# Splitting one ScalarE copy in two and re-spacing the delta-rule levels of a two-block fp32 kernel

## The reference

```python
kk = jnp.einsum("bhncd,bhnjd->bhncj", k, k)
m = jnp.where(strict, beta[..., :, None] * kk * decay, 0.0) + jnp.eye(C, dtype=f32)
rhs = jnp.concatenate([v * beta[..., None], k * (beta * jnp.exp(gc))[..., None]], axis=-1)
sol = lax.linalg.triangular_solve(m, rhs, left_side=True, lower=True, unit_diagonal=True)
...
def step(state, inp):
    u = u0_c - jnp.einsum("bhcd,bhde->bhce", w_c, state)
    o = jnp.einsum("bhcd,bhde->bhce", qd_c, state) + jnp.einsum("bhcj,bhje->bhce", qk_c, u)
    state = cd_c[..., None, None] * state + jnp.einsum("bhcd,bhce->bhde", kd_c, u)
    return state, o
```

## Time and profile before

| | |
|---|---|
| median of 3 runs | 3284.47 us (3281.02 to 3286.4) |
| the profiled execution | 3288.24 us, its span 3286.4 us |
| TensorE matmuls busy | 3119.8 us (95% of the span) |
| VectorE, ScalarE, GpSimd busy | 48%, 26%, 51% |
| chain that ended last | PE 83%, DVE 12%, ACT 3% |
| trips 1 to 12 | about 430 to 1660 us of the span |
| mean DMA rate | 93 GB/s |

### The profile page before, as it was taken

One profiled execution on the slowest core, in us unless ns is written; L12 is line 12 of the kernel. 1 busy time (PEld: TensorE's weight loads), 2 busy tenths in 40 slices (PEclk: granted clock), 3 DMA queues, 4 the chain that ended last, 5 costly groups with the idle time before them and its releaser, 6 DMA issues.

```text
span 3286.4 us, 43215 instructions
## 1 busy us (share of the span) xinstructions
PE 3119.8 (95%) x15168; PEld 2545.6 (77%) x15168; DVE 1566.5 (48%) x2169; ACT 851.4 (26%) x1327; POOL 1684.4 (51%) x1748
## 2 busy tenths in 40 slices
PE   8999989999999999999799999999989999999996
PEld 7877778778778777787688887778768887778685
DVE  6721245555655556555622124344356666530723
ACT  5421133332333323333201011111123333310411
POOL 0255544444444344443357776566645555456774
PEclk9999999999999999999899999999999999999998
DMA  6322222212221221222242223222232212323221
GB/s 244 132 72 92 93 71 77 77 57 70 77 89 64 71 76 68 79 79 75 104 170 90 93 99 134 91 102 89 102 115 80 83 67 83 105 75 128 77 100 79
DMA packets 53527, 306.47 MB, mean 93 GB/s; under 512 B 5044, under 2 KB 7220, under 8 KB 21716
## 3 DMA queue, kind: packets, MB, share of 16 engines
q1 hardware_dynamic: 34528, 248.53, 21.6%
q10 hardware_dynamic: 18932, 57.00, 4.6%
HBM read 284.74 MB, written 20.77 MB: 93 GB/s over the span
## 4 chain that ended last, share of the span: by engine, by line
PE 83%; DVE 12%; ACT 3%; issue 1%; DMA 1%; ACTq 0%; DVEq 0%
PE gemm_ps L424 20%; PE gemm_ps L426 20%; PE gemm_ps L425 20%; DVE arena L859 7%; PE bankC L558 2%; DVE a_lo L859 2%; PE bankA L548 2%; PE gemm_ps L776 2%; PE gemm_ps L778 2%; PE gemm_ps L777 2%; PE bankA L732 2%; ACT arena L1590 2%; DVE arena L865 1%; PE bankB L579 1%; PE bankA L573 1%
## 5 line engine op out<-in xcount | busy, mean ns | idle before, releaser
L424 PE MATMUL gemm_ps<-a_hi,w_hi 128*128 128x512 f32 (+1 forms) x3472 | 1390.3, 400 | 24.1 <-DVE a_lo L859 14.4
L400 POOL CAST w_hi<-w_raw 128x512 fp32r<-128x512 f32 x872 | 538.8, 660 | 1555.1 <-issue 1393.6
L426 PE MATMUL gemm_ps<-a_hi,w_lo 128*128 128x512 f32 (+1 forms) x3472 | 1334.5, 384 | 0.0
L425 PE MATMUL gemm_ps<-a_lo,w_hi 128*128 128x512 f32 (+1 forms) x3472 | 1332.9, 384 | 0.0
L392 POOL TENSOR_TENSOR w_lo<-w_raw,w_hi 128x512 fp32r<-128x512 f32 x872 | 1149.5, 1349 | 4.3
L424 PEld LDWEIGHTS gemm_ps<-a_hi,w_hi 128*128 128x128 f32 x3472 | 659.6, 190 | 158.5 <-issue 24.0
L426 PEld LDWEIGHTS gemm_ps<-a_hi,w_lo 128*128 128x128 f32 x3472 | 656.7, 189 | 131.2
L425 PEld LDWEIGHTS gemm_ps<-a_lo,w_hi 128*128 128x128 f32 x3472 | 659.3, 190 | 121.8 <-issue 9.2
L859 DVE TENSOR_TENSOR arena<-gemm_ps,arena 128x512 f32<-128x512 f32 (+3 forms) x161 | 107.1, 665 | 606.1 <-PE gemm_ps L426 472.7
L1590 ACT ACTIVATE arena<-arena 128x512 f32<-128x512 f32 (+5 forms) x350 | 214.6, 613 | 410.7 <-DVE arena L859 396.0
L859 DVE RECIPROCAL arena<-arena 128x512 f32<-128x512 f32 (+2 forms) x70 | 172.7, 2468 | 249.9 <-ACT arena L1590 247.8
(11 more groups left out here) (168 smaller groups left out, 2571.3 us busy)
## 6 DMA issues: line engine op xcount, KB each, us to landing
w_raw<-w_stream SPq DMA_DIRECT2D x236, 1024.0 KB, 4.8
y_scratch<-arena ACTq DMA_DIRECT2D x20, 512.0 KB, 3.2
arena<-y_scratch ACTq DMA_DIRECT2D x13, 512.0 KB, 3.9
arena<-gc_scratch ACTq DMA_DIRECT2D x12, 512.0 KB, 5.8
arena<-x_t ACTq DMA_DIRECT2D x2, 2048.0 KB, 9.9
arena<-y_scratch ACTq DMA_DIRECT2D x1, 4096.0 KB, 24.5
x_scratch<-arena ACTq DMA_DIRECT2D x1, 4096.0 KB, 14.3
y_out<-arena ACTq DMA_DIRECT2D x4, 1024.0 KB, 3.9
```

Of the source, the lines that this page charges most:

```text
L400: pool.tensor_copy(part(w_hi, w, q), part(w_raw, w, q)).then_inc(pool_step, 1)
L424: pe.matmul(o, hi, a_hi[:, k, 0:width], start=(k == 0), stop=False)
L425: pe.matmul(o, hi, a_lo[:, k, 0:width], start=False, stop=False)
L426: last = pe.matmul(o, lo, a_hi[:, k, 0:width], start=False, stop=(k == KT - 1))
```

## The change

Four things.
1. The product T of a level is written to two PSUM banks, chunks 0 and 1 to bank A's first, 2 and 3 to its second (level 1 keeps both in the first, since the second is still being read). TensorE signals after each pair; ScalarE copies T in two 128x256 activations; `whole` waits for each half on its own.
2. The four column operations behind level 2 go from VectorE to ScalarE, at the head of `values`.
3. `DN_STEPS` gets other weights: `half` 0 in place of 1 everywhere, so that no dense block stands between `half` and `whole`; `values` 13 for 12; at level 5 `whole` 2 for 1 and `turn` 2 for 3; at level 6 `whole` 1 for 2; `head_out` 24 for 18.
4. The step counts per trip follow (57 for 61 and 24 for 20).

```diff
-DN_STEPS = ([("natural", 12), ("values", 12)]
-            + [(s, l, w) for l in range(1, LEVELS - 2) for s, w in (("half", 1), ("whole", 4))]
-            + [("half", LEVELS - 2, 1), ("whole", LEVELS - 2, 1), ("turn", 3)]
-            + [("half", LEVELS - 1, 1), ("whole", LEVELS - 1, 2), ("flip", 2), ("solved", 4)]
+DN_STEPS = ([("natural", 12), ("values", 13)]
+            + [(s, l, w) for l in range(1, LEVELS - 2) for s, w in (("half", 0), ("whole", 4))]
+            + [("half", LEVELS - 2, 0), ("whole", LEVELS - 2, 2), ("turn", 2)]
+            + [("half", LEVELS - 1, 0), ("whole", LEVELS - 1, 1), ("flip", 2), ("solved", 4)]
             + [(s, n, g) for n in range(NB) for s, g in (("rest", 2), ("output", 3))]
-            + [("head_out", 18)])
+            + [("head_out", 24)])
...
+        def half_bank(l, q):
+
+            return bankA[:, q if l > 1 else 0, :]
...
                     for n in range(NB):
-                        last = pe.matmul(quad(bankA)[:, 0, n, :], pair_n[:, n, :], inv_a[:, n, :],
+                        last = pe.matmul(half_bank(l, n // 2)[:, n * P:n * P + P], pair_n[:, n, :], inv_a[:, n, :],
                                          start=True, stop=True)
-                    last.then_inc(s["t1"], 1)
+                        if n % 2:
+                            last.then_inc(s["t1"], 1)
...
                     for n in range(NB):
+                        if n % 2 == 0:
+                            pe.wait_ge(s["t1_sbuf"], 2 * level_count(j, l) - 1 + n // 2)
...
-                    elif l == 2:
-                        op(v.tensor_copy, ke_scale[:, :, 0], cb[:, :, 3, 0])
-                        op(v.tensor_scalar, u_scale[:, :, 0], neg_br[:, :, 0], -1.0, None, ALU.mult)
-                        op(v.tensor_copy, u_scale[:, :, 1], kroot)
-                        op(v.tensor_scalar, neg_k, kroot, -1.0, None, ALU.mult)
...
+                    op(ke_scale[:, :, 0], cb[:, :, 3, 0], ACT.Copy)
+                    op(u_scale[:, :, 0], neg_br[:, :, 0], ACT.Copy, scale=-1.0)
+                    op(u_scale[:, :, 1], kroot, ACT.Copy)
+                    op(neg_k, kroot, ACT.Copy, scale=-1.0)
...
-                    op(chunks(T1, 0), bankA[:, 0, :], ACT.Copy, s["t1_sbuf"], level_count(j, step[1]))
+                    for q in range(2):
+                        done = 2 * level_count(j, step[1]) - 1 + q
+                        act.wait_ge(s["t1"], done if step[1] > 1 else 2 * level_count(j, 1))
+                        op(chunks(T1, 0)[:, q * 256:q * 256 + 256], half_bank(step[1], q)[:, q * 256:q * 256 + 256], ACT.Copy,
+                           s["t1_sbuf"], done)
```

More of the change, by code:

```diff
@@ L547, in dn_mix @@
                     for n in range(NB):
-                        last = pe.matmul(quad(bankA)[:, 0, n, :], pair_n[:, n, :], inv_a[:, n, :],
+                        last = pe.matmul(half_bank(l, n // 2)[:, n * P:n * P + P], pair_n[:, n, :], inv_a[:, n, :],
                                          start=True, stop=True)
-                    last.then_inc(s["t1"], 1)
+                        if n % 2:
+                            last.then_inc(s["t1"], 1)
                 elif step[0] == "whole":
                     l = step[1]
-                    pe.wait_ge(s["t1_sbuf"], level_count(j, l))
                     pe.wait_ge(s["inv_ready"], 2 * level_count(j, l))
@@ L1093, in dn_mix @@
                         op(v.tensor_tensor, dT[:, :, :, :], E[:, :, :, :], both(dTm), ALU.mult)
-                    elif l == 2:
-                        op(v.tensor_copy, ke_scale[:, :, 0], cb[:, :, 3, 0])
-                        op(v.tensor_scalar, u_scale[:, :, 0], neg_br[:, :, 0], -1.0, None, ALU.mult)
-                        op(v.tensor_copy, u_scale[:, :, 1], kroot)
-                        op(v.tensor_scalar, neg_k, kroot, -1.0, None, ALU.mult)
                     elif l == 3:
                         op(v.tensor_tensor, kd[:, :, :, :], both(by_chunk(bankB[:, 0, :])), by_row(kd_scale), ALU.mult)
-                    else:
+                    elif l == 4:
                         op(v.tensor_tensor, ke[:, :, :, :], both(by_chunk(bankB[:, 0, :])), by_row(ke_scale), ALU.mult,
@@ L1761, in dn_mix @@
                 elif step[0] == "half":
-                    act.wait_ge(s["t1"], level_count(j, step[1]))
                     if step[1] == 1:
                         act.wait_ge(s["dy_stored"], 16 * j + 16)
-                    op(chunks(T1, 0), bankA[:, 0, :], ACT.Copy, s["t1_sbuf"], level_count(j, step[1]))
+                    for q in range(2):
[3 more added lines that the diff above has]
+                           s["t1_sbuf"], done)
                 elif (step[0] == "whole" and step[1] < LEVELS - 2) or step[0] == "turn":
@@ L2158 @@
             + [("values", 0)])
-DN_VECTOR_STEPS = 61
-DN_SCALAR_STEPS = 20
+DN_VECTOR_STEPS = 57
+DN_SCALAR_STEPS = 24
 def kernel(**inputs):
```

## The result

| | before | after |
|---|---|---|
| median (4 runs each, side by side) | 3283.2 us | 3257.8 us (3255.16 to 3259.18) |
| ratio, 95% interval | | 0.9922 (0.991 to 0.9934) |
| the profiled execution, its span | 3288.24, 3286.4 us | 3257.62, 3255.8 us |
| start of trip 1, start of trip 12 | 429.74, 1557.21 us | 427.96, 1535.38 us |
| trip 1 | 111.8 us | 109.8 us |

The kernel became 25.4 us faster; 23 were forecast. The two profiled executions lie 30.6 us apart, and the place of each piece can be read: 1.8 us ahead of trip 1 (which the change doesn't touch), 2.0 in trip 1, 18.1 in trips 2 to 11, 8.8 from the start of trip 12 to the end. The distance of the medians, 25.4 us, is what the change is worth; the profiled execution of the kernel before is itself 5.0 us slower than its median here.

What follows compares the result with a forecast made beforehand. TensorE, busy 95% of the span, bounds the kernel; only its idle and half-clock time can be won. Trips -3, clock -14.6, first trip -2.5, last -2.5: about -23 us, from 3284.5 to 3261.5 us, range 3250 to 3277.

Steps and rivals of the forecast that it cites:

- level 1: Level 1, both copies behind all four products: 5.7 to 5.8 us against 5.98, one block less, +0.5 us a trip.
- level 2, level 4: Plain levels, `half` to next `half`: 0.62 us shorter, but one block of 0.675 must go elsewhere, +0.06 each.
- level 3: Level 3 without the column operations on VectorE: 2.12 us less, one block less, -1.45 us a trip.
- level 5: `half` to `turn` at level 5: 3.47 us against 4.03 with as many blocks, -0.55 us a trip.
- `turn` to `solved`: Stretch from `turn` to `solved`: 7.2 us against 8.81, three blocks (2.0) less, +0.4 us a trip.
- behind `solved` (`rest`): State update behind `solved`: no block ahead of `output` 2, so `rest` 3 waits a block more, +0.7 us a trip.
- trip 1: First trip: most of its 11.7 us excess comes ahead of level 1 and stays; -2.5 us for its level 3.
- trip 12: Last trip: the four column operations leave the stretch ahead of the wait for tile 0's bank, -2.5 us.
- The 14.6 us: Excess of ten trips, put down to the clock falling behind the gap ahead of level 4's `half`; all -14.6 us taken.
- Rival A: Levels 1 to 4: clock falls as often as before through several close gaps, the 14.6 us stay, 3276 us; chance 0.16.
- C: ScalarE becomes late, level 1 waits 1.6 us a trip, 19 us in all, 3281 us; chance 0.05.
- B: Levels 1 to 4 run at 1.2 GHz once every trip, 2.7 us each, 3294 us, 0.3% slower; chance 0.09.

Runs made afterwards that it cites:

- cols_split: Kernel after with the old `DN_STEPS` weights restored, split and moved column operations kept: 3222.33 us, ratio 0.9801 to the kernel before.
- undo_cols: Kernel after with the four column operations back on VectorE behind level 2: 3288.47 us, ratio 1.0007 to the kernel before.
- split_only: Kernel before with only T's split into two banks and two copies, old weights, columns on VectorE: 3286.23 us, ratio 0.9998.

## Why the prediction was right, and where it was off

Trip 3 by the prediction's steps; measured is the change of the stretch plus 0.675 us for each block taken out of it:

| step | predicted | measured |
|---|---|---|
| level 1 | +0.5 | 5.75 - 5.98 + 0.675 = +0.45 |
| level 2, level 4 | +0.06 each | 5.08 long: +0.08, +0.09 |
| level 3 | -1.45 | 6.18 - 8.20 + 0.675 = -1.35 |
| level 5 | -0.55 | 3.43 - 4.03 = -0.60 |
| `turn` to `solved` | +0.4 | 7.04 - 8.81 + 2.03 = +0.26 |
| behind `solved` (`rest`) | +0.7 | +0.73 |
| the trip | -0.3 | 100.11 to 99.76: -0.35 |
| trips 2 to 11 | -14.6 - 2.8 = -17.4 | -18.1 |
| trip 1 | -2.8 | -2.0 |
| trip 12 | -2.5 | -8.8 to the end |

**The steady trips** came out as worked out: the signs named (trips near 99.8 and alike, level 3 at 6.1, plain levels at 5.05, `rest` 3 waiting 1.4, clock at 1.00) are there as 99.76, 6.18, 5.08, 1.46 and 1.00 (only trip 1, at 109.8, isn't like the others). The claim that the split "pays for the blocks it displaces and no more" holds for this change: -0.59 us a level against 0.675 for the block. Costing the columns on ScalarE at nothing was right too.

**The 14.6 us were read as the clock's alone, and that is wrong by a third.** The prediction says that the clock falls behind the same gap in other trips, and shows the stretch from 1289.0. That stretch lies in trip 9, whose gap is 3.96 us. The same gap of 2.8 us cost the clock in trips 2, 4 and 6 and left it in trips 3, 5 and 8; in the other four the column operations were 1.2 us longer each time. The term came out whole because one edit, the columns' move, took away both causes, which is partly luck. Rival A, in which only the clock's part stays, should have been priced at 9.8 us and not 14.6. Of trip 1's 11.7 us, too, only 4.1 stand ahead of level 1 (23.63 us to `half` 1 against 19.50); 4.9 are in level 1 itself, where `whole` waits 4.50 us, and 2.6 in levels 2 to 4.

**Trip 12 was mis-sized.** The wait for tile 0's bank fell from 5.97 us to 3.04, near the 2.5 forecast. But `solved` comes 8.8 us earlier (81.8 to 73.0 us behind the trip's start), with six blocks (4.05) displaced behind it: 4.7 net, so about 1.8 us more than I counted. Some 1.1 of that stands ahead of level 1, where `half` waited 5.28 us and waits 3.21. Behind `solved` both kernels take 1647.4 us, although after has those 4 us of blocks more. The clock covers that: from 115 us behind the start of trip 12 to the end, windows at 0.50 cost 14.8 us of matmul time in the kernel before (seven stretches and parts of the last 25 us) and 10.6 in the one after (five, and the same end). That is 4.1 us less in a stretch that the change doesn't touch, where the same loss ranges from 9.7 to 16.0 us over the ten kernels. So I count it as luck, which the forecast had no term for. The ten profiled executions spread from 1718.9 to 1729.2 us between the start of trip 12 and the end, before being the longest. The 1.8 us ahead of trip 1 are of the same kind; the ten kernels start trip 1 between 427.8 and 429.9. These 5.9 us together are about what the two profiled executions lie further apart than the medians (30.6 against 25.4).

**What the prediction didn't ask** is whether the split and the weights belong together. It priced a displaced block at a flat 0.675 and carried it as a mere transfer. `cols_split` shows what each one had covered (trip 3 of both):

| stretch | blocks moved | `cols_split` | after |
|---|---|---|---|
| `natural` to `half` 1 | +1 | 19.50 | 20.18 |
| level 1 | -1 | 5.75 | 5.75 |
| level 2 | -1 | 5.43 | 5.08 |
| level 3 | -1 | 6.19 | 6.18 |
| level 4 | -1 | 5.42 | 5.08 |
| level 5 | 0 | 3.77 | 3.43 |
| `turn` to `solved` | -3 | 8.47 | 7.04 |
| behind `solved` | +6 | 42.3 | 47.0 |

Seven blocks, 4.7 us, left the levels, and the levels became 2.5 us shorter. In levels 1 and 3 the block was free: the chain through ScalarE and VectorE is as long without it. All seven come back at full price, and `rest` waits 0.7 us more. That is the 3.0 us a trip between the two kernels.

**The rivals.** A (the clock falls as often) fell: no half-clock stretch in trips 2 to 11. C (ScalarE late) fell: level 1 took its 5.75 us. B (each trip loses the clock) fell for this change but is real: `undo_cols` and `split_only` do just that, at 1.7 and 2.7 us of matmul time a trip, on either side of the 1.9 from which it was to decide. What keeps it away is the columns' move, not the blocks. The Trainium skill, TensorE: Matmul & The Clock Gate, in Loop structure matters more than you think, has matmuls back-to-back as its good case and a long wait for a DMA between every matmul as its bad one. These kernels lie between the two: gaps of 0.3 to 1.5 us in trips 2 to 11 left the clock at 1.00, and those of 2.3 to 4.2 us ahead of level 4 are where it fell. `undo_cols` has the short gaps of the kernel after and one longer one, so here one long gap did the harm, not many short ones.

**Open.** The stretch at half clock is 3.4 us long behind a gap of 2.3 (`undo_cols`) and 6.8 behind one of 4.2 (`split_only`); in the kernel before a gap of 2.8 us cost the clock in three trips and left it in three. What sets length and luck wasn't tried.

## What to carry to other kernels

When a bundle of edits is timed as one, time the re-spacing apart: here two gains were sold together with new weights that gave back more than half of them. A filler, a dense block dealt in to cover a wait, is free wherever the chain beside it is longer than the block, so move fillers only after the chain was shortened, and out of places whose gap has closed, one gap at a time. And look at what the neighbour engine does when a tiny operation is slow, and at the operation in every trip and not in one: its length can jump when everything around it moves by hundredths of a microsecond. The cheapest cure is to run it at another moment, or with an operand elsewhere.

## What the hardware showed that I had not expected

- A VectorE copy or scaling of 128x4 took 0.17 us with GpSimd idle, and up to 1.28 us while GpSimd was splitting weights; as a `scalar_tensor_tensor` with one operand in PSUM it took 0.16 at the same place. I had taken the 2.54 us of the four for their own length; it was 2.54 in six of the ten steady trips and 3.7 in the other four.
- ScalarE does the same operation in 207 ns with a constant scale; the row of 298 ns that I had taken has a third operand, `eps`.
- Making a chain shorter ahead of such operations can make them longer and cost the clock: in `split_only` they took 3.75 us in all ten steady trips, the gap was 4.2 us, half clock took 6.8 us of every trip from the third, and the gain of the levels was gone.
